# Seven of the last stage's fifteen loading places served by GpSimd's DMA queue

## What is computed

```
h = x + y @ w_out
t = rmsnorm(h)
for e in 32 experts:                     # two experts chosen per token
    h = h + combine[:, e] * ((silu(t @ w1[e]) * (t @ w3[e])) @ w2[e])
pe   = rmsnorm(p @ w_ple)
gate = sigmoid(rmsnorm(h) @ w_pg + b_pg)
out  = h + gate * pe
```

## Time and profile before

| | us |
|---|---|
| median of 3 runs | 1387.04 |
| lowest, highest | 1386.98, 1390.51 |
| the profiled execution | 1388.14 |
| its span, first to last instruction | 1386.1 |
| TensorE matmuls busy | 1089.3 (79%) |
| DVE busy | 285.3 (21%) |
| ScalarE busy | 156.7 (11%) |
| GpSimd busy | 53.4 (4%) |
| DMA, mean over the span | 344 GB/s, 476.14 MB |

### The profile page before, as it was taken

How to read it: one execution, slowest core, us unless ns; L and a number is a source line. 1 busy time by engine, 2 the same in 40 slices (tenths; PEclk the granted TensorE clock), 3 DMA queues, 4 the chain that set the end, 5 groups by cost and what they waited for, 6 DMA issues and landing times.

```text
span 1386.1 us, 13825 instructions
## 1 busy us (share of the span) xinstructions
PE 1089.3 (79%) x6016; PEld 504.8 (36%) x6016; DVE 285.3 (21%) x439; ACT 156.7 (11%) x314; POOL 53.4 (4%) x66
## 2 busy tenths in 40 slices
PE   8999999999876686666765667666576656989998
PEld 4458887445522232222222223222232212333333
DVE  1104726412321212121221121000000000111116
ACT  1111315002200011000000000000000000010102
POOL 0112110200000002000000000000000000000000
PEclk9999999999888899788898788888888877999999
DMA  9943334354599999999999999999999999999961
GB/s 351 305 152 122 122 122 147 129 217 182 227 426 426 429 426 427 429 426 428 429 426 428 428 426 426 415 427 428 414 427 415 427 428 409 384 395 387 397 267 61
DMA packets 91053, 476.14 MB, mean 344 GB/s; under 512 B 10272, under 2 KB 10416, under 8 KB 67952
## 3 DMA queue, kind: packets, MB, share of 16 engines
q1 hardware_dynamic: 84896, 471.88, 84.1%
q0 software_dynamic: 560, 2.88, 0.6%
q10 hardware_dynamic: 5536, 0.47, 0.3%
HBM read 473.12 MB, written 2.10 MB: 343 GB/s over the span
## 4 chain that ended last, share of the span: by engine, by line
DMA 50%; PE 47%; SPq 1%; DVE 1%; issue 1%; ACT 0%; DVEq 0%
DMA ring<-in_w 48%; PE ps L1421 8%; PE ps L1384 6%; PE ps L1851 6%; PE ps L1674 5%; PE ps L1754 4%; PE ps L1545 4%; PE ps L1558 4%; PE ps L1809 2%; DMA area<-in_w 2%; PE ps L1646 2%; PE ps L1822 1%; PE ps L1639 1%; SPq L386 1%; PE ps L1578 1%
## 5 line engine op out<-in xcount | busy, mean ns | idle before, releaser
L1754 PE MATMUL ps<-ring,area 128*32 128x512 f32 x1024 | 166.4, 796 | 122.6 <-DMA ring<-in_w 122.0
L1674 PE MATMUL ps<-ring,area 128*32 128x512 f32 x976 | 147.7, 724 | 126.2 <-DMA ring<-in_w 126.2
L1184 DVE TENSOR_TENSOR h<-ps,h 128x2048 f32<-128x2048 f32 x32 | 73.3, 2292 | 298.8 <-PE ps L1646 298.8
L1754 PEld LDWEIGHTS ps<-ring,area 128*32 128x32 f32 x1024 | 43.1, 139 | 232.3 <-issue 232.3
L1421 PE MATMUL ps<-hT,ring 128*128 128x256 f32 x512 | 112.9, 380 | 0.0
L1674 PEld LDWEIGHTS ps<-ring,area 128*32 128x32 f32 x976 | 31.6, 122 | 222.7 <-issue 222.4
L1421 PEld LDWEIGHTS ps<-hT,ring 128*128 128x128 f32 x512 | 96.5, 190 | 14.0 <-issue 1.2
L1851 PE MATMUL ps<-ring,area 128*128 128x512 f32 x192 | 88.6, 603 | 6.3 <-DMA ring<-in_w_pg 4.9
L1384 PE MATMUL ps<-ring,hT 128*128 128x512 f32 x192 | 85.0, 602 | 1.1 <-DVE hT L907 1.1
L1229 DVE TENSOR_TENSOR hT<-area,ps 128x128 f32<-128x128 f32 x16 | 4.6, 288 | 315.8 <-ACT area L860 315.8
L1639 PE MATMUL ps<-area,hs 128*128 128x128 f32 x512 | 66.2, 284 | 0.5 <-DVE area L1165 0.5
(11 more groups left out here) (278 smaller groups left out, 775.0 us busy)
## 6 DMA issues: line engine op xcount, KB each, us to landing
ring<-in_w SPq DMA_DIRECT2D x157, 2048.0 KB, 21.5
ring<-in_w SPq DMA_DIRECT2D x57, 1024.0 KB, 15.1
ring<-in_w_in SPq DMA_DIRECT2D x28, 1024.0 KB, 12.6
ring<-in_w_out SPq DMA_DIRECT2D x16, 1024.0 KB, 7.2
ring<-in_w_pg SPq DMA_DIRECT2D x12, 1024.0 KB, 15.7
area<-in_w SPq DMA_DIRECT2D x2, 2048.0 KB, 14.0
hs<-in_w SPq DMA_DIRECT2D x4, 1024.0 KB, 14.3
hs<-in_w_pg SPq DMA_DIRECT2D x3, 1024.0 KB, 17.4
```

What stands on the lines that cost most here:

```text
L1184: dve.tensor_tensor(h[:, t, :], ps[:, bank:bank + 4, :].rearrange("p b n -> p (b n)"), h[:, t, :], ALU.add).then_inc(acc_done, 1)
L1674: ins = mm(ps[SLOTS * g:SLOTS * g + SLOTS, 0, :], XG[:, b, k, SLOTS * e:SLOTS * e + SLOTS], s[:, D_EXP * kk:D_EXP * kk + D_EXP], start=(k ...
L1754: ins = mm(ps[SLOTS * g:SLOTS * g + SLOTS, 0, :], XG[:, b, k, SLOTS * e:SLOTS * e + SLOTS], s[:, D_EXP * kk:D_EXP * kk + D_EXP], start=(k ...
```

## The change

`late_loads(queue, half)` holds the two old load functions in one and walks the same 64 loads in the same order, with the same places, counts and semaphores. Each load whose place is in `POOL_PLACES` is begun by GpSimd, the others by SP. `POOL_PLACES` comes out as (3, 5, 7, 9, 12, 13, 14): 30 of the 64 loads go to GpSimd, 34 stay with SP. Of the first eleven loads, numbered 0 to 10, GpSimd has 0, 1, 2, 4, 6, 8 and 10. The bias load moves from GpSimd to SP, behind SP's last of the 34.

```diff
+POOL_PLACES = tuple(s for s in range(PLACES) if s >= RING or s % 2 and s not in (slot_of(33), slot_of(35)))
...
+        def late_loads(queue, half):
+            for what, i, q, k in piece_loads():
+                place, after, _ = PLACED[what, i, q, k]
+                if (place in POOL_PLACES) != (half == 1):
+                    continue
+                queue.wait_ge(open_used, after)
+                if what == "w2":
+                    e = FULL + QUAD * q
+                    queue.dma_start(places[place].rearrange("p (e n) -> p e n", e=QUAD),
+                                    w2_v[e:e + QUAD, :, k, 512 * i:512 * i + 512].rearrange("e p n -> p e n")
+                                    ).then_inc(open_loaded[place], 16)
+                else:
+                    queue.dma_start(places[place], w_pg_v[:, 4 * i + q, :]).then_inc(open_loaded[place], 16)
...
@@ SP, after the pairs of quad 3
-            for what, i, q, k in piece_loads():
-                if what == "w2":
-                    w2_piece_load(i, q, k)
-                else:
-                    w_pg_load(i, q)
-
+            late_loads(sp_q, 0)
+            sp_q.wait_ge(open_used, OPEN_CHUNKS - 4)
+            sp_q.dma_start(bpg, b_pg.partition_broadcast(P).rearrange("p a d -> p (a d)")).then_inc(bpg_loaded, 16)
             for u in range(2 * 4):
@@ GpSimd
             pool.tensor_tensor(r_ple[:, :], ss[:, 4:6], expo[:, 0:2], ALU.pow).then_inc(rp_ready, 1)
-            pool.wait_ge(open_used, OPEN_CHUNKS - 4)
-            pool.dma_start(bpg, b_pg.partition_broadcast(P).rearrange("p a d -> p (a d)")).then_inc(bpg_loaded, 16)
+            late_loads(pool, 1)
             norm_root(3)
```

## The result

| | before | after |
|---|---|---|
| median, us | 1387.01 (4 runs) | 1399.09 (4 runs, 1397.1 to 1402.1) |
| ratio | | 1.0077, 95% interval 1.006 to 1.0093 |
| span of the profiled execution | 1386.1 | 1397.1 |

The change costs 12.1 us (0.8%). I had forecast 1390.5, 3.4 us more than before; the side was right, the size was not, and 1399.1 lies 1.1 us above the top of my range. Executions of one program are not all alike: of the four of before three took 1387.0 and one 1390.5 us, so a single profile can stand some 4 us off its median.

A forecast was written before the change was run, and what follows sets the result against it. DMA alone was taken to bound quad 3, DMA and TensorE nearly level the last stage. Quad 3 15.0 us later, less 11.6 regained, gave +3.4 us: 1390.5 us after adjusting to the median and rounding, range 1383.5 to 1398.0.

The forecast's parts named there:

- the share of the queues at quad 3's end: At quad 3's end: GpSimd's and SP's queues each get about half; quad 3 ends 15.0 us later (7.4 + 9.6 - 2).
- The reading of the bottleneck: In quad 3 and the last stage: the DMA engines are full, so a second issuer changes only the order of loads.
- The first three w_pg: Before quad 3's end: begun some 80 us early on GpSimd, they make quad 3's last loads 7.4 us later.
- the bias: Leaving the crowded stretch, it ends quad 3 2 us earlier and makes all later loads 2.5 us earlier.
- the issue costs: On GpSimd: 0.8 us per load at most, 24 for 30 loads, beside idle time.
- Loads 4, 6, 8 and 10: At quad 3's end: they run beside its last w2 loads with half the share, delaying them 9.6 us.
- my upper bound of 16.3 us: Quad 3's end if all four loads go in front: 7.4 + 10.9 - 2 us later.
- The sum for the last stage: After quad 3: TensorE, starting 15 us later, meets no late load and gains 11.6 us; net +3.4 us.
- C: Rival, last stage: the mixture is slower or GpSimd's loads come late; at 10% rate lost +11.5 us, 1398.5; chance 0.22.
- A: Rival: GpSimd's loads give way to quad 3's or are issued late enough; -2.5 us, 1384.5; chance 0.14.
- B: Rival: two queues carry 2 KB rows better and GpSimd's loads give way at quad 3's end; -6.2 us, 1381; chance 0.12.

The follow-up runs named there:

- experiment 3: The kernel before, with only the first three w_pg loads begun by GpSimd and the bias last on SP: 1385.94 us, ratio 0.9983.
- experiment 2: The kernel before, with all 64 loads kept on SP and only the gate bias moved to SP behind them: 1385.76 us, ratio 0.9987.
- experiment 5: The changed kernel, with GpSimd's loads after its first three w_pg held until quad 3's last w2 chunk has landed: 1395.04 us, ratio 1.005.
- the change twice: The changed kernel as first measured, 1399.09 us, and a second series with no edit, 1401.92 us, 14.7 us later than before.
- experiment 4: The changed kernel, with all of GpSimd's loads held until quad 3's last w2 chunk has landed: 1393.26 us, ratio 1.0047.
- experiment 6: The changed kernel, with slots 0, 4 and 8 also on GpSimd (42 of 64 loads), all its loads held behind quad 3: 1389.35 us, ratio 1.0014.
- 7: The changed kernel, GpSimd's loads except the first three w_pg waiting for higher counts: four higher 1394.71 us (1.0048), two higher 1391.76 us (1.0027).
- experiment 1: A separate kernel that only loads, from SP and GpSimd in phases; with 2 KB rows SP alone 388 GB/s, GpSimd alone 387, both 385.

## Why the prediction missed the size

Two steps failed, both to the same side, so that nothing cancelled: the share of the queues at quad 3's end (17.6 us later for 15.0), and the last stage (7.3 us won back for 11.6).

**The reading of the bottleneck** held. A second issuer brought no byte: 391, 388 and 396 GB/s in the three stretches from 1227 to 1325 us, for 396, 391 and 393 before.

**The first three w_pg** held: 8.1 us later at quad 3's end between experiments 3 and 2, 7.2 when the marks (0.84 us apart) are taken off, for 7.4. So did the bias (1.8 for 2.5, inside the interval), and the issue costs.

**Loads 4, 6, 8 and 10**: the first step that failed is "Against these GpSimd's 2 KB packets get half". That the share goes by packet was right, and shown; that GpSimd's packets hold one row was taken over from SP's rows. They hold two. The trace of before has no 2 KB rows on q0, but it could have told that this queue packs short rows: over 36 to 50 us it moved the four loads of w_a and w_i, 2048 rows of 256 B, in 192 packets of 2.7 KB, more than ten rows each:

```profile
q0 software_dynamic: 192, 0.52, 15.2%
```

The Trainium skill ("DMA: Bandwidth & Descriptors", SWDGE vs HWDGE vs iDMA) says that a packet there is preferably up to 4096 B; the 3.87 KB agree, and I had not drawn on it. With two thirds the four loads are wholly in front of quad 3's end, my upper bound of 16.3 us; measured 18.3, or 17.6 with the mark's 0.7 taken off. The bytes agree: from the mark to quad 3's last chunk GpSimd's queue moved 7.34 MB, all seven of its loads, and all queues together 46.30 MB for 39.40 before. These 6.90 MB take 16.5 us at 417 GB/s; the other 1.1 us are the mean rate itself, 417 for 422 GB/s, since more of it went in short rows. Both queues were to have near half after 1160 us; GpSimd's had two thirds.

**The sum for the last stage**, the second step that failed: "a TensorE that starts 15 us later never meets a late load. It gains the whole 11.6" failed. It took for granted that DMA stays full and that loads land in their order. Neither did: DMA lost 6.5 us for want of free places, and 2.5 MB passed a load of SP's that TensorE then waited for. Both are shown in the changed kernel's trace. That order alone costs, with DMA full, is shown by experiment 5 beside 3 (3.66 MB passed, 9.5 of 10.2 us). Whose loads are late bears it out: in the four profiles with the changed kernel's split and no later counts (the change twice, experiments 4 and 5) all 15 w2 chunks that TensorE waits for in the last stage are SP's. That it is the ratio of share to need is only argued: experiment 6 made the two equal and the later waits stayed as long. How the 14.7 us divide exactly is not settled: the kernels 4, 5 and 7 each take off 7 to 10 us, and these overlap.

**The rivals.** C had the side and nearly the size, by the wrong means: the rate with DMA busy did not fall, and the loads that came late were SP's, not GpSimd's. The hold of GpSimd's descriptors by DVE that the Trainium skill tells of ("SBUF — State Buffer", the box on DVE blocking DMA) shows nowhere: a w2 load's issue on GpSimd takes 0.75 us here, as in experiment 1 (7.4 to 7.6 us for ten), where DVE does nothing. A and B fell: nothing of GpSimd's gave way against short rows. Had order not mattered, the result would have been the bias's.

**Versions that beat both**: the bias alone and the first three on GpSimd, 0.13% and 0.17% faster than before. The first three add nothing clear to the bias (1385.94 and 1385.76 us), and the split of the other loads only costs.

## What to carry to other kernels

Where the DMA engines are full, a second queue does not add bandwidth; it gives up the order of need that one queue keeps for nothing, and replaces it by a share per packet. Before splitting a stream, look at packets and MB of each queue in a stretch where both run, with the rows that will be moved. Giving each queue the part of the loads that it gets of the bytes made the loss smaller here (2.1 and 5.3 us for 12.1 and 14.7, with GpSimd's loads held behind quad 3), but did not beat one queue. And a load moved ahead is free only as long as DMA stays full and the load is itself wanted before the last wait that it delays: the first three, moved by 80 us, cost nothing here; with the other 27 split off as well it came to 12 to 15 us.

## What the runs showed of the hardware that I had not expected

GpSimd's queue packs two 2 KB rows into one packet (3.87 KB mean), SP's does not (2.0 KB); with 8 KB rows each row is a packet in both (7.3 KB mean over both queues in the 8 KB phase, the shortest packets counted in), and SP's 16 KB rows go in packets of 14.6 KB. Rows of 256 B went some ten to a packet on GpSimd's queue (2.7 KB mean). Packets of 3.9 KB move no more than packets of 2.0 KB: 387 against 388 GB/s, while 8 KB rows give 17.34 MB in 41 us, 423 GB/s. So in these phases the rate goes with the length of the row, and the share with the length of the packet. And 14.6 KB packets of SP's left GpSimd's short rows a fifth of the bytes: the same queue is the strong one or the weak one, depending on its neighbour's rows.
